# First units of an expert pair in halves, down weights by column halves and column chunks in turn

## The chip, the cores and the metric

The kernel runs on one core of one Trainium2 chip. The metric is the time of one execution on the device in microseconds (us), as the median of several runs. One further execution was profiled; all rows below are of that one.

## The reference

One layer of a transformer trunk for 384 tokens (128 context tokens, 256 latent ones) of width 2048, all in float32: modulated norm, a joint input projection for three groups of heads, attention, an output projection with a gated residual, and then a mixture of experts, which is the part that changes:

```python
g_top_p, g_top = top_k(softmax(h @ w_rg + b_rg), 1)           # 4 groups
e_logit, e_top = top_k((h @ w_re + b_re)[group g_top], 2)     # 2 of the 8 experts of a group
e_w = softmax(e_logit) * g_top_p
# 32 experts, each token goes to two; per expert e and its tokens x:
y = (silu(x @ w1[e]) * (x @ w3[e])) @ w2[e]                   # w1, w3: 2048 x 512, w2: 512 x 2048
out = x1 + g2 * sum over the token's two experts of e_w * y
```

Each expert has 12.6 MB of weights, all of which must be read once.

## The kernel before, in words

The stages ahead of the experts take the first 728 us or so. Then the tokens of each expert are put into items of up to 64 tokens, and items are worked in pairs: expert A fills rows 0 to 63 of the output partitions and expert B rows 64 to 127, so each step of a pair is two matmuls (one for each expert), and a float32 matmul shows as two instructions. There are 16 pairs in this run. The first is written out by hand with weights in 24 units of 1 MiB, and it is `moe0` in the code. The other 15 use 12 units of 2 MiB each, six slots of the tile `ring`, slot = unit % 6: units 0 to 3 are w1 (rows j = 0 to 7 of A and of B, then j = 8 to 15), 4 to 7 are w3 likewise, 8 to 11 are w2 (f = 0 and 1 of A and of B, then f = 2 and 3). A partition of a unit of w1 holds 8 steps j of 512 columns, 16 KB; one of w2 holds 2 rows f of 2048 columns, 16 KB, taken out of 32 KB in memory. Fourteen pairs are a hardware loop over m, the last is written out behind it.

Who does what in a pair:

- SyncE issues the loads in the order of the units and ahead of each waits until the slot is free (`moe_free`, lines 811 to 819; the loop, lines 876 to 882). Landing adds 16 to `big_full` of the slot, on which TensorE waits (`moe_arrived`).
- TensorE: `up` (lines 1376 to 1392) makes h1 and h3, 16 steps j each, and waits for two units when j is 0 or 8. From j = 5 of w1 on, one "back" of the pair before stands behind every second step (12 in all, line 1297): it spreads that pair's result over the tokens, three bfloat16 matmuls each on parts that ACT and DVE split off. Then `turn_next` transposes the gathered rows of the next pair, `turn_act` the activations, and the down-projection (lines 1410 to 1426) runs with f outside and the four column chunks c of 512 inside, one PSUM bank for each chunk. A chunk is complete after f = 3, and `y_full` counts it.
- ACT and DVE read h1, h3 and the complete chunks (`front`, `parts`), and GpSimd gathers the token rows of the pair after the next with an indirect DMA.

Behind the loop, the last pair (lines 1429 to 1454) has f = 0 and 1 for all chunks first, and then for each chunk f = 2 and 3, followed by the last backs of the chunk before (`last_back`, line 1402, float32, three matmuls a chunk on tiles that DVE has gated). DVE adds a strip to the residual for each, and SyncE stores it in pieces of 256 KB.

The lines that set the present order of the down-projection:

```python
for f in range(4):
    ua, ub = 8 + f // 2 * 2, 9 + f // 2 * 2
    if f % 2 == 0:
        moe_arrived(ua, m)
        moe_arrived(ub, m)
    for c in range(4):
        for h, u in enumerate((ua, ub)):
            mm = pe.matmul(y_ps[c][64 * h:64 * h + 64, :], act_t[:, f, 64 * h:64 * h + 64],
                           big_cut(slot_of(u), (2, D))[:, f % 2, c * 512:(c + 1) * 512], ...)
```

Of the kernel before, what the change touches and what calls it, by code (L numbers as in the profile page):

```python
# [18 lines left out]
I32 = mybir.dt.int32  # L19
# [5 lines left out]
P = 128  # L25
# [31 lines left out]
SCRATCH = 8192  # L57
BACKS = 4 * TILES
# [297 lines left out]
def by_units(w_mod, b_mod, w_in, w_o):  # L356
# [15 lines left out]
def build(nc, ins, outs):  # L372
# [54 lines left out]
    with ExitStack() as ctx:  # L427
# [22 lines left out]
        n_items = sb("n_items", [1, 1], I32)  # L450
# [209 lines left out]
        extra_full = [sem(f"extra_full{i}") for i in range(EXTRA[1] - EXTRA[0] - 1)]  # L660
        extra_free, strip_scaled = sem("extra_free"), sem("strip_scaled")
# [23 lines left out]
        def unit_source(u, e=0):  # L685
# [31 lines left out]
            w = ins["w2"][0][bass.ds(e, 1)]  # L717
            return w.rearrange("e (p j) n -> p (e j) n", j=4)[:, 2 * half:2 * half + 2, :], (2, D)
# [82 lines left out]
        moe_done = {3: (h1_full, 1), 7: (h3_full, 1), 11: (y_full, 4)}  # L801
# [26 lines left out]

        @block.sync
        def _(sp):  # L830
            for t in range(TILES):
# [36 lines left out]
            for u in range(MOE_UNITS):  # L868
# [5 lines left out]
                src, shape = unit_source(("moe", u), e[u % 2])  # L874
                sp.dma_start(big_cut(slot_of(u), shape), src).then_inc(big_full[slot_of(u)], 16)
            with sp.Fori(0, n) as m:
                e = [sp.value_load(expert_of[0:1, bass.ds(2 * m + 4 + c, 1)], min_val=0, max_val=EXPERTS - 1)
                     for c in range(2)]
                for u in range(MOE_UNITS):
                    sp.wait_ge(*(moe_free(u + BIG, m) if u < BIG else moe_free(u - BIG, m + 1)))  # L880
                    src, shape = unit_source(("moe", u), e[u % 2])
                    sp.dma_start(big_cut(slot_of(u), shape), src).then_inc(big_full[slot_of(u)], 16)
# [12 lines left out]
        def _(pe):  # L895
# [464 lines left out]
            for f in range(4):  # L1360
                ua, ub = 16 + 2 * f, 17 + 2 * f
                first_arrived(ua)
                first_arrived(ub)
                for c in range(4):
                    if f == 0 and c == 2:
                        pe.wait_ge(xt_read_a, 4)
                        pe.wait_ge(xt_read_v, 4)
                    for h, u in enumerate((ua, ub)):
                        mm = pe.matmul(y_ps[c][64 * h:64 * h + 64, :], act_t[:, f, 64 * h:64 * h + 64],  # L1369
                                       first_place(u)[:, c * 512:(c + 1) * 512], start=(f == 0), stop=(f == 3))  # L1370
                        if u == FIRST_UNITS - 1:
                            mm.then_inc(y_full, 1)
                        elif c == 3 and u in first_no:
                            mm.then_inc(slot_free[ring_slot(first_no[u])], 1)

            def up(m):
# [29 lines left out]
            with pe.Fori(0, n) as m:  # L1406
# [3 lines left out]
                for f in range(4):  # L1410
# [4 lines left out]
                    for c in range(4):  # L1415
                        if f == 0 and c == 2:
                            pe.wait_ge(xt_read_a, m * 2 + 6)
                            pe.wait_ge(xt_read_v, m * 2 + 6)
                        for h, u in enumerate((ua, ub)):
                            mm = pe.matmul(y_ps[c][64 * h:64 * h + 64, :], act_t[:, f, 64 * h:64 * h + 64],  # L1420
                                           big_cut(slot_of(u), (2, D))[:, f % 2, c * 512:(c + 1) * 512],
                                           start=(f == 0), stop=(f == 3))
                            if f == 3 and u in moe_done:
                                mm.then_inc(y_full, 1)
                            elif f % 2 and c == 3:
# [6 lines left out]
            def last_down(c, f):  # L1432

                for h in range(2):
                    mm = pe.matmul(y_ps[c][64 * h:64 * h + 64, :], act_t[:, f, 64 * h:64 * h + 64],  # L1435
                                   big_cut(slot_of(8 + f // 2 * 2 + h), (2, D))[:, f % 2, c * 512:(c + 1) * 512],
                                   start=(f == 0), stop=(f == 3))
                return mm

            moe_arrived(8, n)  # L1440
            moe_arrived(9, n)
            for f in range(2):
                for c in range(4):
                    last_down(c, f)
            moe_arrived(10, n)
            moe_arrived(11, n)
            for c in range(4):
                last_down(c, 2)
                last_down(c, 3).then_inc(y_full, 1)
                if c == 1:  # L1450
                    pe.wait_ge(w_ready, n + 2)
                if c:
                    last_back(n, c - 1)
# [967 lines left out]
```

## Time and profile before

| what | us |
|---|---|
| median of 3 runs | 1681.74 (1680.48 to 1683.66) |
| the profiled execution | 1681.13 |
| its span in the profile | 1679.3 |
| TensorE busy with matmuls | 1574.7 (94%) |
| DVE, ACT, GpSimd busy | 737.8, 281.0, 102.5 |

The span is the time from the first to the last instruction of the profiled execution; 1.8 us of its time lie around it. Busy times of several engines overlap. In the rows PE is TensorE, SPq the DMA-issuing queue of SyncE, and L1387 is line 1387 of the kernel: L1387 and L1346 are matmuls of the up-projection, L1420, L1369 and L1435 those of the down-projection, L1297 and L1402 the backs. All weights of the experts appear as `ring<-in_w`.

### The profile page before, as it was taken

How to read it: one execution, taken by the hardware profiler on the slowest of the kernel's cores; microseconds unless marked ns; L12 is line 12 of the kernel's file. 1: busy time of each engine (PE TensorE's matmuls, PEld its weight loads, DVE VectorE, ACT ScalarE, POOL GpSimd, SP SyncE). 2: the span in 40 equal slices, each digit the busy share in tenths (PEclk: the TensorE clock that was granted, in tenths of full speed). 3: DMA queues.
4: the chain of work that ended last, by engine and by line, in shares of the span. 5: the costliest groups of instructions: out<-in, count | busy, mean ns of one | idle time of the engine just before them, and what ended most of it. 6: DMA issues, size and time to landing. Idle time of an engine off the chain costs nothing.

```text
span 1679.3 us, 18083 instructions
## 1 busy us (share of the span) xinstructions
PE 1574.7 (94%) x6570; PEld 648.0 (39%) x6615; DVE 737.8 (44%) x1392; ACT 281.0 (17%) x744; POOL 102.5 (6%) x189
## 2 busy tenths in 40 slices
PE   6999999999999999999999899899989989989998
PEld 3446555544434444443332332333233233233323
DVE  3583333113255993344444445444434434544444
ACT  3014222112132000011101111110110111011010
POOL 1002100000022001010000000000000000000000
PEclk9999999999999999999999999999999999999999
DMA  9993345526199765699999999999999999999996
GB/s 394 420 415 130 117 187 223 206 107 251 57 380 415 278 262 202 234 376 426 424 429 428 428 428 427 425 428 426 427 428 422 426 428 424 429 425 428 425 426 250
DMA packets 60109, 581.93 MB, mean 347 GB/s; under 512 B 8993, under 2 KB 9953, under 8 KB 15179
## 3 DMA queue, kind: packets, MB, share of 16 engines
q1 hardware_dynamic: 52832, 557.34, 80.0%
q0 software_dynamic: 5936, 23.23, 3.6%
q10 hardware_dynamic: 1296, 0.77, 0.2%
q8 instruction: 27, 0.44, 0.1%
q14 instruction: 18, 0.15, 0.0%
HBM read 584.07 MB, written 7.05 MB: 352 GB/s over the span
## 4 chain that ended last, share of the span: by engine, by line
PE 68%; DMA 16%; DVE 4%; issue 2%; ACT 1%; SPq 0%; POOL 0%; ACTq 0%
PE bank L1387 24%; DMA ring<-in_w 16%; PE bank L1131 13%; PE bank L1297 7%; PE bank L1109 7%; PE bank L1420 3%; DVE r L1920 2%; PE bank L1004 2%; PE bank L1222 2%; PE bank L1346 2%; PE bank L1283 1%; PE bank L1435 1%; PE bank L1369 1%; PE bank L1197 1%; PE bank L1205 1%
## 5 line engine op out<-in xcount | busy, mean ns | idle before, releaser
L1387 PE MATMUL bank<-ring,r 128*64 128x512 f32 x1920 | 466.3, 615 | 45.3 <-DMA ring<-in_w 45.3
L1387 PEld LDWEIGHTS bank<-ring,r 128*64 128x64 f32 x1920 | 128.9, 139 | 300.6 <-issue 300.6
L2147 DVE TENSOR_TENSOR bank<-bank,r 128x512 f32<-128x512 f32 x180 | 126.0, 700 | 262.8 <-PE bank L1297 262.8
L1131 PE MATMUL bank<-ring,r 128*128 128x384 f32 (+2 forms) x672 | 225.4, 494 | 0.0
L1420 PE MATMUL bank<-ring,mod_row 128*64 128x512 f32 x896 | 195.8, 593 | 8.0 <-ACT mod_row L1655 7.9
L1109 PE MATMUL bank<-ring,r 128*128 128x512 f32 x384 | 170.0, 595 | 0.0
L1131 PEld LDWEIGHTS bank<-ring,r 128*128 128x128 f32 x672 | 123.6, 190 | 90.9 <-issue 43.2
L1297 PE MATMUL bank<-r 128*128 128x512 bf16 x495 | 137.6, 382 | 7.2 <-issue 7.2
L2149 DVE TENSOR_TENSOR r<-r,bank 128x512 f32<-128x512 f32 x180 | 123.6, 687 | 6.2
L1420 PEld LDWEIGHTS bank<-ring,mod_row 128*64 128x64 f32 x896 | 75.1, 137 | 119.1 <-issue 108.9
L1297 PEld LDWEIGHTS bank<-r 128*128 128x128 bf16 x540 | 38.0, 97 | 167.4 <-DVE r L2149 97.4
L1109 PEld LDWEIGHTS bank<-ring,r 128*128 128x128 f32 x384 | 71.1, 191 | 79.5 <-issue 79.4
L2170 DVE TENSOR_SCALAR gains<-bank,w_now 128x512 f32<-128x512 f32 x30 | 22.5, 751 | 175.3 <-PE bank L1420 162.3
L951 PE MATMUL bank<-r 128*128 128x512 f32 (+1 forms) x192 | 78.6, 558 | 5.1 <-DMA r<-in_w_cq 5.1
L2003 DVE TENSOR_REDUCE small<-bank 128x1 f32<-128x384 f32 (+1 forms) x48 | 22.5, 468 | 127.9 <-PE bank L1197 77.3
L1920 DVE SCALAR_TENSOR_TENSOR r<-ring,csil,r 128x2048 f32<-128x2048 f32 x32 | 74.3, 2349 | 6.3 <-DMA r<-in_b_mod 5.7
L1948 DVE SCALAR_TENSOR_TENSOR r<-r,small,gains 128x128 f32<-128x128 f32 (+2 forms) x91 | 27.4, 343 | 109.7 <-POOL small L2265 100.7
L1644 ACT ACTIVATE r<-bank 128x512 f32<-128x512 f32 x30 | 17.9, 595 | 301.7 <-PE bank L1283 301.7
L1764 DVE CUSTOM_DVE_ANT_0 r<-ring,r 128x2048 bf16<-128x2048 f32 x24 | 56.4, 2351 | 1.3
L1525 ACT ACTIVATE r<-bank 128x128 f32<-128x128 f32 (+1 forms) x76 | 21.0, 285 | 210.4 <-PE bank L1131 195.8
L1650 ACT ACTIVATE gain_row<-bank 128x512 f32<-128x512 f32 x16 | 9.6, 597 | 275.1 <-PE bank L1387 261.4
L951 PEld LDWEIGHTS bank<-r 128*128 128x128 f32 x192 | 35.6, 193 | 47.5 <-issue 32.5
(291 smaller groups left out, 1245.5 us busy)
## 6 DMA issues: line engine op xcount, KB each, us to landing
ring<-in_w SPq DMA_DIRECT2D x180, 2048.0 KB, 17.5
ring<-in_w_mod SPq DMA_DIRECT2D x64, 1024.0 KB, 11.6
ring<-in_w SPq DMA_DIRECT2D x18, 1024.0 KB, 9.0
ring<-in_w_scale SPq DMA_DIRECT2D x16, 1024.0 KB, 26.9
ring<-in_w_shift SPq DMA_DIRECT2D x16, 1024.0 KB, 26.7
ring<-in_w_o SPq DMA_DIRECT2D x16, 1024.0 KB, 6.3
r<-mod_d POOLq DMA_DIRECT2D x8, 1024.0 KB, 8.5
ring<-in_w_aq SPq DMA_DIRECT2D x8, 768.0 KB, 14.2
```

The source lines that it names most:

```text
L951: mm = pe.matmul(early_bank[3 * c + t][:, 0:w], h_t[:, k, t * P:(t + 1) * P], early_w[c][i % 2][:, jj, :], start=(k == 0), stop=(k == KD - 1))
L1004: mm = pe.matmul(mod_ps[32 * q:32 * q + 2, :], csil[:, k, 0:2], ring[:, ring_slot(m), q * 512:(q + 1) * 512], start=(k == 0), stop=(k == K ...
L1109: mm = pe.matmul(acc[acc_of(a)][:, :], qo[:, t, k, :], wu[:, j, :], start=(k == 0), stop=(k == KD - 1))
L1131: mm = pe.matmul(acc[acc_of(a)][:, 0:w], h_t[:, k, t * P:(t + 1) * P], wu[:, j, :], start=(k == 0), stop=(k == KD - 1))
L1222: mm = pe.matmul(out, v, prob_t[u % 2][:, i, :] if g == "C" else prob_ab[batch_of(u) % 2][:, i, :], start=(i == 0), stop=(i == len(tiles) ...
L1297: mm = pe.matmul(y_ps[k % 4][:, :], of_token[:, t * P:(t + 1) * P], y_part[:, n_part, c, :], start=(n_part == 0), stop=(n_part == 2))
L1387: mm = pe.matmul(ps[64 * c:64 * c + 64, :], xg_t[:, j, 64 * c:64 * c + 64], big_cut(slot_of(u), (8, 512))[:, j % 8, :], start=(j == 0), st ...
L1420: mm = pe.matmul(y_ps[c][64 * h:64 * h + 64, :], act_t[:, f, 64 * h:64 * h + 64], big_cut(slot_of(u), (2, D))[:, f % 2, c * 512:(c + 1) * ...
L1764: last = v.tensor_tensor_reduce(junk_s, w, cond_all[:, c, :], 1.0, b_shift[:, k:k + 1], ALU.mult, ALU.add, mod_t[:, 1, k, c:c + 1])
L1920: last = v.scalar_tensor_tensor(out=g2_sum[:, c, :], in0=ring[:, ring_slot(m), :], scalar=csil[:, k, c:c + 1], in1=g2_sum[:, c, :], op0=AL ...
L2147: v.tensor_tensor(ps[:, :], ps[:, :], g2b[:, min(t, 1), cols], ALU.mult).then_inc(strip_scaled, 1)
L2149: return v.tensor_tensor(x1[:, t, cols], x1[:, t, cols], ps[:, :], ALU.add)
```

## The change

The weights w2 are laid out anew in memory on the host, outside the timed execution: for each expert two dense blocks of 2 MiB, one for columns 0 to 1023 and one for 1024 to 2047, in each of which a partition holds chunk after chunk and in a chunk f after f. A unit of w2 is then a column half with all four f. The down-projections run with c outside and f inside, and `y_full` counts each chunk when it is complete, so unit 9 and the odd units of the first pair have `y_full` for the sign that they are free. Units 0 and 1 of each of the 15 pairs are loaded in halves, in the order 0a, 1a, 0b, 1b; the first halves have semaphores of their own (`half_full`, the reused `early_in`), and `up` waits for them at j = 0 and for the whole units at j = 4. SyncE's loop ends one pair earlier, and the last pair's loads are written out behind it, w2 in eight transfers of 1 MiB, chunk by chunk, counted in `last_full`. The last pair's down-projection waits for each chunk and runs chunk by chunk.

```diff
+    down = w2[0].reshape(EXPERTS, P, 4, 2, 2, 512)
+    out["w2"] = down.transpose(0, 3, 1, 4, 2, 5).reshape(EXPERTS, 2, P, 2 * D)
...
-                return ins["w2"][0][n % 2].rearrange("(p j) n -> p j n", j=4)[:, (n - 16) // 2, :], (D,)
+                c = (n - 16) // 2
+                return ins["w2"][n % 2, c // 2][:, c % 2 * D:c % 2 * D + D], (D,)
...
-            w = ins["w2"][0][bass.ds(e, 1)]
-            return w.rearrange("e (p j) n -> p (e j) n", j=4)[:, 2 * half:2 * half + 2, :], (2, D)
+            w = ins["w2"][bass.ds(e, 1), half]
+            return w.rearrange("e p (c n) -> p (e c) n", c=2), (2, D)
+
+        def last_source(e, c):
+
+            w = ins["w2"][bass.ds(e, 1), c // 2]
+            return w.rearrange("e p n -> p (e n)")[:, c % 2 * D:c % 2 * D + D]
...
-            elif u == FIRST_UNITS - 1:
-                frees[m] = (y_full, 4)
+            elif u > 16 and u % 2:
+                frees[m] = (y_full, (u - 15) // 2)
...
-        moe_done = {3: (h1_full, 1), 7: (h3_full, 1), 11: (y_full, 4)}
+        moe_done = {3: (h1_full, 1, 1), 7: (h3_full, 1, 1), 9: (y_full, 4, 2), 11: (y_full, 4, 4)}
...
-                full, n = moe_done[u]
-                return full, m * n + 2 * n
+                full, each, at = moe_done[u]
+                return full, m * each + each + at
...
+            def load_big(u, e):
+
+                src, shape = unit_source(("moe", u), e[u % 2])
+                if u > 1:
+                    sp.dma_start(big_cut(slot_of(u), shape), src).then_inc(big_full[slot_of(u)], 16)
+                    return
+                sp.dma_start(big_cut(slot_of(u), shape)[:, 0:4, :], src[:, 0:4, :]).then_inc(half_full[u], 16)
+                for c in range(2 * u):
+                    src, shape = unit_source(("moe", c), e[c])
+                    sp.dma_start(big_cut(slot_of(c), shape)[:, 4:8, :], src[:, 4:8, :]).then_inc(big_full[slot_of(c)], 16)
...
-            with sp.Fori(0, n) as m:
+                load_big(u, e)
+            before_last = sp.value_load(n_items[0:1, 1:2], min_val=HALF_PAIR - 3, max_val=MAX_PAIRS - 3)
+            with sp.Fori(0, before_last) as m:
...
-                    src, shape = unit_source(("moe", u), e[u % 2])
-                    sp.dma_start(big_cut(slot_of(u), shape), src).then_inc(big_full[slot_of(u)], 16)
+                    load_big(u, e)
...
+            for u in range(8):
+                sp.wait_ge(*(moe_free(u + BIG, before_last) if u < BIG else moe_free(u - BIG, before_last + 1)))
+                load_big(u, e)
+            for c in range(4):
+                for h in range(2):
+                    if c % 2 == 0:
+                        sp.wait_ge(*moe_free(2 + c + h, before_last + 1))
+                    sp.dma_start(big_cut(slot_of(8 + c // 2 * 2 + h), (2, D))[:, c % 2, :],
+                                 last_source(e[h], c)).then_inc(last_full[c], 16)
...
-                        if j % 8 == 0:
+                        if w == 0 and j == 0:
+                            for c in range(2):
+                                pe.wait_ge(half_full[c], m * 16 + HALF_FULL + 16)
+                        elif j % 8 == (4 if w == 0 and j < 8 else 0):
                             moe_arrived(ua, m)
                             moe_arrived(ub, m)
...
-                for f in range(4):
-                    ua, ub = 8 + f // 2 * 2, 9 + f // 2 * 2
-                    if f % 2 == 0:
-                        moe_arrived(ua, m)
-                        moe_arrived(ub, m)
-                    for c in range(4):
-                        if f == 0 and c == 2:
-                            pe.wait_ge(xt_read_a, m * 2 + 6)
-                            pe.wait_ge(xt_read_v, m * 2 + 6)
-                        for h, u in enumerate((ua, ub)):
+                for c in range(4):
+                    if c == 2:
+                        pe.wait_ge(xt_read_a, m * 2 + 6)
+                        pe.wait_ge(xt_read_v, m * 2 + 6)
+                    if c % 2 == 0:
+                        moe_arrived(8 + c, m)
+                        moe_arrived(9 + c, m)
+                    for f in range(4):
+                        for h in range(2):
+                            u = 8 + c // 2 * 2 + h
                             mm = pe.matmul(y_ps[c][64 * h:64 * h + 64, :], act_t[:, f, 64 * h:64 * h + 64],
-                                           big_cut(slot_of(u), (2, D))[:, f % 2, c * 512:(c + 1) * 512],
+                                           big_cut(slot_of(u), (2, D))[:, c % 2, f * 512:(f + 1) * 512],
                                            start=(f == 0), stop=(f == 3))
-                            if f == 3 and u in moe_done:
+                            if f == 3 and h == 1:
                                 mm.then_inc(y_full, 1)
...
+            def last_down(c):
+
+                pe.wait_ge(last_full[c], 16 + 2 * 16)
+                for f in range(4):
...
+            last_down(0)
+            last_down(1)
+            pe.wait_ge(w_ready, n + 2)
+            last_back(n, 0)
+            last_down(2)
+            last_back(n, 1)
+            last_down(3)
+            last_back(n, 2)
             last_back(n, 3)
```

The diff is cut: the first pair's down-projection is turned in the same way as that of the loop, and `n_items` gets a second value, one less than the first.

## Rows read from the trace of the kernel before

**Rows 1.** The page, section 2: what the DMA engines moved in 40 slices.

```profile
GB/s 394 420 415 130 117 187 223 206 107 251 57 380 415 278 262 202 234 376 426 424 429 428 428 428 427 425 428 426 427 428 422 426 428 424 429 425 428 425 426 250
```

**Rows 2.** Waits of TensorE and SyncE's queue: us in total, times, longest.

```profile
PE bank L1387 <- DMA ring<-in_w: 45.3, 20, 3.4
PE bank L1297 <- issue: 7.2, 45, 0.2
...
SPq L882 <- PE bank L1387: 522.4, 56, 12.0
```

**Rows 3.** Timeline, TensorE: start, us, instructions [idle before, releaser].

```profile
889.87 7.07 PE L1387 MATMUL bank<-ring,r 128*64 128x512 f32 x24 [3.06 <-DMA ring<-in_w]
...
949.88 5.37 PE L1387 MATMUL bank<-ring,r 128*64 128x512 f32 x24 [2.77 <-DMA ring<-in_w]
...
959.66 1.94 PE L1387 MATMUL bank<-ring,r 128*64 128x512 f32 x8 [1.03 <-DMA ring<-in_w]
...
992.57 14.26 PE L1420 MATMUL bank<-ring,mod_row 128*64 128x512 f32 x64 [0.56 <-ACT mod_row L1655]
1009.88 7.07 PE L1387 MATMUL bank<-ring,r 128*64 128x512 f32 x24 [3.06 <-DMA ring<-in_w]
...
1608.61 5.37 PE L1387 MATMUL bank<-ring,r 128*64 128x512 f32 x24 [1.59 <-DMA ring<-in_w]
...
1618.38 1.94 PE L1387 MATMUL bank<-ring,r 128*64 128x512 f32 x8 [1.03 <-DMA ring<-in_w]
```

**Rows 4.** Windows of 20 us; last three columns: granted clock, DMA share, GB/s.

```profile
940.00:960.00 20.00, 16.04 (x73) 5.68 (x72) 9.36 (x14) 6.25 (x10) 0.00 (x0) 1.00 1.01 430
...
1000.00:1020.00 20.00, 16.79 (x69) 5.80 (x66) 8.06 (x12) 6.25 (x10) 0.00 (x0) 0.91 1.01 430
...
1040.00:1060.00 20.00, 19.27 (x96) 7.85 (x95) 7.08 (x13) 1.47 (x3) 1.19 (x2) 1.00 1.00 419
```

**Rows 5.** DMA queues from 940 to 1000 us.

```profile
DMA packets 1887, 25.65 MB, mean 428 GB/s; under 512 B 296, under 2 KB 296, under 8 KB 296
```

**Rows 6.** DMA issues of the whole run: size of each, median us to landing.

```profile
ring<-in_w SPq DMA_DIRECT2D x180, 2048.0 KB, 17.5
...
out_y_prompt<-r SPq DMA_DIRECT2D x4, 256.0 KB, 2.4
```

**Rows 7.** Windows ahead of the loop, columns as in rows 4.

```profile
730.00:760.00 30.00, 30.00 (x154) 12.17 (x150) 6.89 (x28) 1.49 (x3) 2.53 (x5) 1.00 1.01 423
...
40.00:60.00 20.00, 20.00 (x78) 8.23 (x77) 4.87 (x4) 0.00 (x0) 0.64 (x1) 0.98 1.02 423
100.00:120.00 20.00, 18.10 (x61) 8.73 (x58) 15.53 (x16) 2.65 (x6) 3.31 (x6) 1.00 1.02 410
```

**Rows 8.** The chain that ended last, its end: start, us, what.

```profile
1650.38 7.09 PE bank L1435 x32
...
1657.49 3.65 PE bank L1435 x16
1661.14 2.77 PE bank L1402 x6
1663.91 1.87 PE bank L1435 x8
...
1670.42 5.36 PE bank L1402 x12
```

**Rows 9.** Line L882 from 1590 to 1640 us: ns, min, median, max.

```profile
L882 SPq DMA_DIRECT2D ring<-in_w x12: 333/333/381, 1590.2 to 1639.1; - x12
...
DMA to landing us min/median/max: 13.1/16.8/20.8
```

**Rows 10.** Timeline, DVE, the gating of one chunk of the last pair.

```profile
1659.46 1.41 DVE L2211 SCALAR_TENSOR_TENSOR r<-bank,w_now,r 128x512 f32<-128x512 f32 x2 [8.79 <-PE bank L1435]
```

**Rows 11.** Windows of 5 us in the last stage, columns as in rows 4.

```profile
1650.00:1655.00 5.00, 4.62 (x22) 1.96 (x24) 0.67 (x3) 0.30 (x1) 0.00 (x0) 1.00 0.83 354
1655.00:1660.00 5.00, 4.99 (x24) 1.78 (x22) 0.54 (x1) 0.00 (x0) 0.00 (x0) 1.00 0.09 36
```

More of the change, by code:

```diff
@@ L57 @@
 SCRATCH = 8192
+HALF_FULL = 64
 BACKS = 4 * TILES
@@ L353, in units_of, with by_units @@
     return [("in", name, i) for i in range(KD // rows_of(name))]
-def by_units(w_mod, b_mod, w_in, w_o):
+def by_units(w_mod, b_mod, w_in, w_o, w2):
     out = {}
@@ L449, in build @@
         small = sb("small", [P, 90])
-        n_items = sb("n_items", [1, 1], I32)
+        n_items = sb("n_items", [1, 2], I32)
         gat_now = sb("gat_now", [P, 1], I32)
@@ L660, in build @@
         extra_full = [sem(f"extra_full{i}") for i in range(EXTRA[1] - EXTRA[0] - 1)]
+        last_full = extra_full[0:4]
         extra_free, strip_scaled = sem("extra_free"), sem("strip_scaled")
@@ L880, in _ @@
                     sp.wait_ge(*(moe_free(u + BIG, m) if u < BIG else moe_free(u - BIG, m + 1)))
-                    src, shape = unit_source(("moe", u), e[u % 2])
-                    sp.dma_start(big_cut(slot_of(u), shape), src).then_inc(big_full[slot_of(u)], 16)
+                    load_big(u, e)
+            e = [sp.value_load(expert_of[0:1, bass.ds(2 * before_last + 4 + c, 1)], min_val=0, max_val=EXPERTS - 1)
+                 for c in range(2)]
+            for u in range(8):
[7 more added lines that the diff above has]
+                                 last_source(e[h], c)).then_inc(last_full[c], 16)
             for k in range(BACKS):
@@ L1409, in _ @@
                 turn_act(m)
-                for f in range(4):
-                    ua, ub = 8 + f // 2 * 2, 9 + f // 2 * 2
-                    if f % 2 == 0:
-                        moe_arrived(ua, m)
-                        moe_arrived(ub, m)
-                    for c in range(4):
-                        if f == 0 and c == 2:
-                            pe.wait_ge(xt_read_a, m * 2 + 6)
-                            pe.wait_ge(xt_read_v, m * 2 + 6)
-                        for h, u in enumerate((ua, ub)):
+                for c in range(4):
+                    if c == 2:
+                        pe.wait_ge(xt_read_a, m * 2 + 6)
[4 more added lines that the diff above has]
+                    for f in range(4):
+                        for h in range(2):
+                            u = 8 + c // 2 * 2 + h
                             mm = pe.matmul(y_ps[c][64 * h:64 * h + 64, :], act_t[:, f, 64 * h:64 * h + 64],
-                                           big_cut(slot_of(u), (2, D))[:, f % 2, c * 512:(c + 1) * 512],
+                                           big_cut(slot_of(u), (2, D))[:, c % 2, f * 512:(f + 1) * 512],
                                            start=(f == 0), stop=(f == 3))
-                            if f == 3 and u in moe_done:
+                            if f == 3 and h == 1:
                                 mm.then_inc(y_full, 1)
-                            elif f % 2 and c == 3:
+                            elif f == 3 and c % 2:
                                 mm.then_inc(big_free[slot_of(u)], 1)
@@ L1430, in _ @@
             turn_act(n)
[L1432 to L1453, printed above, removed]
+            def last_down(c):
+                pe.wait_ge(last_full[c], 16 + 2 * 16)
+                for f in range(4):
+                    for h in range(2):
+                        mm = pe.matmul(y_ps[c][64 * h:64 * h + 64, :], act_t[:, f, 64 * h:64 * h + 64],
+                                       big_cut(slot_of(8 + c // 2 * 2 + h), (2, D))[:, c % 2, f * 512:(f + 1) * 512],
+                                       start=(f == 0), stop=(f == 3))
+                mm.then_inc(y_full, 1)
+            last_down(0)
[6 more added lines that the diff above has]
+            last_back(n, 2)
             last_back(n, 3)
@@ L2131, in _ @@
             v.tensor_scalar(n_items[:, 0:1], n_extra[0:1], float(HALF_PAIR - 2), None, ALU.add)
+            v.tensor_scalar(n_items[:, 1:2], n_extra[0:1], float(HALF_PAIR - 3), None, ALU.add)
             v.wait_ge(tab_full, 1)
@@ L2408 @@
     arrays = {f"in_{n}": np.ascontiguousarray(inputs[n]) for n in IN_NAMES
-              if n not in ("w_in", "w_o") and n not in dict(GAIN_ROWS)}
-    for n, a in by_units(inputs["w_mod"], inputs["b_mod"], inputs["w_in"], inputs["w_o"]).items():
+              if n not in ("w_in", "w_o", "w2") and n not in dict(GAIN_ROWS)}
+    for n, a in by_units(inputs["w_mod"], inputs["b_mod"], inputs["w_in"], inputs["w_o"],
+                         inputs["w2"]).items():
         arrays[f"in_{n}"] = np.ascontiguousarray(a)
```

16 lines of the change are left out of this document (8 added, 8 removed).

## The prediction

> **What bounds the kernel now.** The page first: one core, and in nearly every slice of the second half of the span 422 to 429 GB/s are moved [rows 1], while TensorE is busy nearly all the time as well. Shares can't say which of the two sets the pace of the expert pairs, so I went on to the waits. TensorE waits for weights in the up-projection 20 times, 45.3 us in all; the queue of SyncE in its turn waits for TensorE to free slots, 522.4 us in the biggest of its groups [rows 2]. So each waits for the other, and the list alone would allow a loop in which a shorter wait of TensorE starts transfers earlier. The timeline of TensorE settles the pace [rows 3]: the first matmul of a pair starts at 889.87, 949.88 and 1009.88, every 60.0 us, whatever TensorE did in between (the wait before it was 3.06, 2.77 and 3.06 us, the first 24 matmul instructions took 7.07 or 5.37 us). A pace that takes no notice of TensorE is that of the other side. The windows by 20 us agree: DMA share 1.00 to 1.01 and 419 to 430 GB/s in each [rows 4]. One pair is 12 units of 2 MiB, 25.17 MB, with the gathered rows 25.65 MB between 940 and 1000 [rows 5]; at 428 GB/s that is 59.9 us. And a unit lands 17.5 us after its issue (median) while 2 MiB take 4.9 us at 428 GB/s, so over three are in flight: the queue's waits for slots don't empty the DMA engines [rows 6].
>
> So from about 730 us, where the DMA share reaches 1.0 [rows 7], until the last landing that TensorE waits for, time is bytes over rate. That landing is at 1618.2 us: the second unit-pair of the last pair (units 2 and 3, needed at j = 8), where TensorE waits 1.03 us [rows 3]. The chain of waits from there on holds no DMA: the steps from j = 8 with the backs of the pair before, the transposition, the 64 instructions of the down-projection, last backs to 1675.78, then one DVE strip and its store [rows 8]. The span is therefore (last wait ends, 1618.38) + 60.9 us in which TensorE or what it must wait for is never short of weights.
>
> **The change part by part.**
>
> *First units in halves.* Units 0 and 1 (both experts' w1, first half) come as 1 MiB pieces, first halves of both, then second halves. Both units together take 4.19 MB / 428 = 9.8 us, so the first halves land 4.9 us before unit 1 lands now. Take the pair at 1009.88: TensorE ended the down-projection at 992.57 + 14.26 = 1006.83 and waited for a landing at about 1009.7. The first halves would be there at 1004.8: no wait. The 16 instructions of j = 0 to 3 take about 3.5 us (5.37 for 24), to 1010.5, and the second halves are there at 1009.7: no wait either. From the first matmul to the end of j = 7 TensorE needs 959.66 - 1.03 - 949.88 = 8.75 us, so it stands at j = 8 at 1006.98 + 8.75 = 1015.7. There units 2 and 3 are next, and they land at 959.5 + 60 = 1019.5 as now. So the wait is moved, not removed: 2.77 + 1.03 = 3.80 us in two places become about 3.8 us in one. After it everything is at its old time; worth 0. The cover is the DMA engines' work itself; were it gone, the wait's whole length would be won (a rival below).
>
> *What else follows the earlier start.* The backs of the pair before (from j = 5) come some 4.9 us earlier in that pair and need split parts that ACT and DVE can finish only after y_full; the next edit gives the first y_full earlier, so nothing stands there. Slots of units 0 and 1 come free some 3 us earlier; the queue has over three units in flight already, 0.
>
> *More and smaller transfers.* Two more issues per pair on SyncE: an issue instruction is 0.33 us, and 12 issues spread over 49 us, 1590.2 to 1639.1 [rows 9], so the queue has room. The second half of unit 0 now also waits for unit 7's slot (one 0.2 us matmul later), with 13.1 us or more from issue to landing in which earlier transfers run [rows 9]. What isn't hidden is any loss of rate on the pieces of 8 KB per partition where there were 16 KB. Bytes: units 0 and 1 of 15 pairs, 62.9 MB, 147 us at 428 GB/s. The nearest rows are the stretch where the very first pair's 1 MiB units (8 KB per partition) load at full share: 423 GB/s [rows 7], against 428 for the 2 MiB units [rows 5]. At 423 the loss is 147 x (428/423 - 1) = 1.7 us; but in that stretch two broadcasts on the software queue run as well, so some of the difference is theirs. Lower end 0. I take the middle, +0.8 us. The Trainium skill ("DMA: Bandwidth & Descriptors", Bandwidth) gives a 1 MB transfer 341 GB/s and 16 MB 425 GB/s and asks to batch; by 341 on the halves the sum would be 147 x (428/341 - 1) = 37 us higher. The trace doesn't agree for transfers in a full queue: the 1 MiB units ran at 423 there.
>
> *w2 by column halves, from memory.* Each unit stays 2 MiB in 16 KB runs per partition, now dense instead of every second 16 KB. The 126 MB of 15 pairs are 294 us of transfer. No row of before has dense 16 KB runs. The first pair's w1 units (8 KB out of every 32 KB) at 423 and the early dense scale and shift units (8 KB, dense) at 423 are equal [rows 7], so I take 0; the bounds are one per cent either way on 294 us, -2.9 and +2.9 us.
>
> *Column chunks in turn.* The same 64 instructions with the same weight loads; y_full for chunk 0 and 1 comes 7 to 10 us earlier, for chunk 3 when it did, so ACT and DVE start on the parts earlier and end the last ones as before. The first two units of w2 are free halfway as before (after 32 of 64 instructions), the others at the end. TensorE doesn't wait for the parts now: what its backs wait for in front of them is issue, 0.2 us at most [rows 2]. 0. The wait for the readers of the transposed rows at chunk 2 comes 5 us later in the stage than it did: 0, since none is seen there now.
>
> *SyncE's last pair written out behind the loop, one more value loaded.* A few register instructions and one load on a queue with 13 us of transfers under way, 0.
>
> *The last pair's down-projection.* Before: 32 + 16 instructions, then back 0, 8, back 1, 8, backs 2 and 3: 7.09 + 3.65 + 2.77 + 1.87 + 2.77 + 1.87 + 5.36 = 25.38 us, without a gap [rows 8]. After: chunks 0 and 1 (7.1), back 0 (2.77), chunk 2 (3.65), back 1 (2.77), chunk 3 (3.65), backs 2 and 3 (5.36) = 25.3. Is it still gapless? Chunks 0 and 1 are at 1654.0 and 1657.5; DVE gates chunk 0 in 1.41 us [rows 10], done 1655.5, so back 0 at 1657.5 finds it with 2 us in hand. Back 3 at 1673.0 needs chunk 3, full at 1670.3, gated at 1671.8. The weights: the last unit lands about 1654 (354 GB/s in 1650 to 1655, then 36 [rows 11]); chunk 2 is wanted at 1660.1 and chunk 3 at 1666.5. So the stores of the first columns leave some 3.5 us earlier and the last ones when they did: -0.1 us. These 8 KB pieces lie behind the last wait for weights and cost nothing.
>
> Sum: 0 + 0.8 + 0 + 0 + 0 - 0.1 = +0.7 us on the profiled execution, 1681.13 (span 1679.3 and 1.8 around it): 1681.8. The median of the runs, 1681.74, is 0.6 above that execution, so 1682.4.
>
> **Rivals.**
>
> *The split pays in full.* If the transfers were paced by slots that TensorE frees, each wait before the first matmul would be won: thirteen, of which rows 3 show the first (3.06) and the last (1.59), with a sum of 38.0 us: 1644 us. For it: the queue does wait for TensorE, 522.4 us in one group [rows 2]. Against it: DMA share 1.0 in the windows [rows 4] and the even 60.0 us. It would need DMA gaps that no window shows. Chance 0.03.
>
> *Dense w2 is faster.* It decides from 3.4 / 294 = 1.15% on these units; at 1.5% -4.4 us and with +0.7 it gives 1678. For it: only that w2 is a third of the bytes. Against: 423 and 423. 0.06.
>
> *Small pieces cost more (the other side).* From a rate below 428 / (1 + 3.4/147) = 418 GB/s on the halves it is slower; at 410, the lowest full-share window of the early stage [rows 7], 6.5 us, 1688. For it: that row. Against: it holds transfers of much smaller pieces too. 0.09. Its extreme is a fixed cost per transfer paid in the DMA engines: a 256 KB store takes 2.4 us from issue to landing [rows 6], of which the bytes are 0.6, so 1.8 us x 2 x 15 = +54 us, 1736; that the 1 MiB units run at 423 speaks against it. 0.01. The Trainium skill ("DMA: Bandwidth & Descriptors", Anatomy of one DMA) has such a fixed cost of about 2.0 us and puts most of it down to the receipt of the last write; the store's 1.8 us agree with the size, and no row shows it taken from a full queue's rate.
>
> *The clock falls in the last pair.* After waits of 3.06 us the first 24 instructions took 7.07 instead of 5.37 us and the granted clock was 0.91 in that window; after 2.77 and 1.59 us they took 5.37 [rows 3, 4]. With one wait of 3.8 us this now happens right behind j = 8; inside the loop it shortens the next wait and costs nothing, in the last pair it lengthens the chain by 1.7 us: 1684.1. There the wait should be 2.6 us at most (1.59 + 1.03), below those that were followed by a fall. 0.15, and still within 0.2%.
>
> *The last pair stalls on a chunk.* If a chunk came 12 us late; nothing in the queue does that. Under 0.01.
>
> **How the numbers follow.** 0.2% of the median, 3.4 us, is about what a measurement of this kernel tells from no change (the three runs spread 3.2 us). The forecast, 1682.4, has 0.63, its own range 1680.6 to 1684.2 from the bounds of the small pieces (0 to 1.7) and of the runs' spread. With the fallen clock (0.15) no measurable change has 0.78. Faster: 0.03 + 0.06 and 0.01 for the unforeseen, 0.10. Slower: 0.09 + 0.01 and 0.02 for a wait that I don't see, 0.12. The rest of w2's bounds widens the range a little on both sides: 1679.3 to 1685.6.
>
> **What would show it.** In the profile after: the first matmul of a pair right behind the down-projection and no wait there; one wait of 2 to 4 us per pair at j = 8; 60.0 to 60.2 us from one such wait's end to the next; DMA share 1.0; in the last stage no gap of TensorE and the end at 1676. A period under 59.5 us, or DMA share below 1 at any place, would make the prediction wrong; a period of 60.3 or more would be the small pieces.

## The result, and the profile after

The changed kernel took 1686.64 us (median of 20 runs, 1683.92 to 1689.98), the kernel before 1683.38 us in the 20 runs beside them (1680.48 to 1686.75). The ratio is 1.0017, 95% interval 1.0011 to 1.0023: slower by 2.9 us, 1.9 to 3.9. The forecast was +0.7 us and 1682.4, with a range to 1685.6. Of the 4.2 us between forecast and result, 2.2 are the effect of the change (+2.9 instead of +0.7), 1.6 are the reference (1681.74 was the median of three runs; over 20 it is 1683.38), and the rest, 0.4, is the difference between ratio and medians.

The profiled execution took 1685.34 us, with a span of 1683.5 (before: 1681.13 and 1679.3). Timeline of TensorE, four of the 14 waits for weights in it, the first three and the last; all 14 stand at j = 8 (start, us, instructions, [idle before, releaser]):

```profile
842.10 1.94 PE L1424 MATMUL bank<-ring,r 128*64 128x512 f32 x8 [1.30 <-DMA ring<-in_w]
...
902.26 3.68 PE L1424 MATMUL bank<-ring,r 128*64 128x512 f32 x8 [4.44 <-DMA ring<-in_w]
...
962.40 3.20 PE L1424 MATMUL bank<-ring,r 128*64 128x512 f32 x8 [1.85 <-DMA ring<-in_w]
...
1622.76 1.94 PE L1424 MATMUL bank<-ring,r 128*64 128x512 f32 x8 [1.90 <-DMA ring<-in_w]
```

The waits of [rows 3] at the start of a pair are gone, and one of 1.3 to 4.5 us at j = 8 stands in for them. The list of waits puts a sum to it, 42.5 us in 14 waits for 45.3 us in 20 of [rows 2]:

```profile
PE bank L1424 <- DMA ring<-in_w: 42.5, 14, 4.5
```

From the first such wait's end to the last one's are 1622.76 - 842.10 = 780.66 us; in before it was 1618.38 - 839.64 = 778.74 us (the last is in [rows 3], the first is this row of the same timeline), so +1.9 us in 13 pairs.

```profile
839.64 1.94 PE L1387 MATMUL bank<-ring,r 128*64 128x512 f32 x8 [1.05 <-DMA ring<-in_w]
```

The DMA queues from 940 to 1000 us, beside [rows 5], show what is new there: 280 more packets for no more bytes. Of them 31 are small ones, under 512 B. The other 249 fit the two units of the pair that now come in halves: each of their 128 partitions gets two runs of 8 KB (a run is what lies in one piece in memory and goes to one partition) instead of one of 16 KB, 256 runs more.

```profile
DMA packets 2167, 25.56 MB, mean 426 GB/s; under 512 B 327, under 2 KB 327, under 8 KB 327
...
ring<-in_w SPq DMA_DIRECT2D x4, 1024.0 KB, 14.0
```

The end of the chain, beside [rows 8]:

```profile
1654.76 7.09 PE bank L1474 x32
1661.84 2.77 PE bank L1439 x6
1664.62 3.58 PE bank L1474 x16
1668.20 2.77 PE bank L1439 x6
1670.97 3.58 PE bank L1474 x16
1674.56 5.36 PE bank L1439 x12
```

From 1654.76 to 1679.92 are 25.2 us without a gap (25.4 before), and from the last wait for weights to the end of the span 60.7 us (60.9 before). The new order of the last pair does what was forecast for it.

The other 2.5 us between the two profiled executions lie ahead of the first wait at j = 8, which ends at 842.10 instead of 839.64, and 2.3 of them lie ahead of all changed code. The last 16 of the matmuls that pick the first pair's rows out of the tokens ("picking matmuls" from here on) start that much later, first in before, then in the changed kernel:

```profile
719.33 7.11 PE L1090 MATMUL bank<-r,cst 128*128 128x512 f32 x16
...
721.63 7.11 PE L1124 MATMUL bank<-r,cst 128*128 128x512 f32 x16
```

In the 8 picking matmuls ahead of these the granted clock fell. Windows of 5 us (columns as in rows 4), first of the changed kernel, then of before:

```profile
710.00:715.00 5.00, 3.89 (x31) 3.27 (x30) 3.04 (x9) 1.32 (x3) 1.46 (x2) 0.88 0.93 324
715.00:720.00 5.00, 5.00 (x9) 2.42 (x9) 4.02 (x16) 0.00 (x0) 0.00 (x0) 0.50 0.95 377
```

```profile
715.00:720.00 5.00, 4.79 (x22) 2.29 (x22) 4.09 (x16) 0.00 (x0) 0.28 (x1) 1.00 1.00 392
```

At 0.50 of full speed (the lower of the clock's two levels, 1.2 GHz) this stage ends later, and SyncE's next weight loads, which come behind a wait for it, start 2.3 us later too, first in before, then in the changed kernel:

```profile
731.97 9.33 SPq L856 DMA_DIRECT2D ring<-in_w  x6
...
734.27 9.33 SPq L879 DMA_DIRECT2D ring<-in_w  x6
```

Since everything behind is bound by transfers, the delay stays to the end.

### The profile page after: what moved, and what is told of

Same layout as the page of the kernel before. It is cut to its first block, busy times and chain, and to the rows that moved or that the text cites. A ratio compares the mean times of both kernels' runs of the same rounds, so it can differ in the third digit from the quotient of the medians.

```text
span 1683.5 us, 18288 instructions
## 1 busy us (share of the span) xinstructions
PE 1590.6 (94%) x6615; PEld 652.5 (39%) x6615; DVE 737.6 (44%) x1393; ACT 281.0 (17%) x744; POOL 102.4 (6%) x189
## 4 chain that ended last, share of the span: by engine, by line
PE 69%; DMA 15%; DVE 4%; issue 1%; ACT 1%; SPq 0%; POOL 0%; ACTq 0%
PE bank L1424 21%; DMA ring<-in_w 15%; PE bank L1165 13%; PE bank L1331 7%; PE bank L1143 7%; PE bank L1457 6%; DVE r L1953 2%; PE bank L1038 2%; PE bank L1317 2%; PE bank L1256 2%; PE bank L1380 2%; PE bank L1474 1%; PE bank L1403 1%; PE bank L1124 1%; PE bank L1231 1%
## 5 line engine op out<-in xcount | busy, mean ns | idle before, releaser
L1424 PE MATMUL bank<-ring,r 128*64 128x512 f32 x1920 | 469.7, 618 | 42.5 <-DMA ring<-in_w 42.5
L1331 PE MATMUL bank<-r 128*128 128x512 bf16 x540 | 150.7, 389 | 0.0
```

The lines of the kernel that those rows point to most:

```text
L1331: mm = pe.matmul(y_ps[k % 4][:, :], of_token[:, t * P:(t + 1) * P], y_part[:, n_part, c, :], start=(n_part == 0), stop=(n_part == 2))
L1424: mm = pe.matmul(ps[64 * c:64 * c + 64, :], xg_t[:, j, 64 * c:64 * c + 64], big_cut(slot_of(u), (8, 512))[:, j % 8, :], start=(j == 0), st ...
```

## The experiments

Eleven further runs were made: nine more kernels, and both old ones once more. They ran on several chips; each ratio is against runs of before made beside that kernel. So that the chance of the early stage doesn't blur the profiles, three stretches are read from each: from the start of the last 16 picking matmuls (about 720 us) to the end of the span ("pick to end"); from the end of the first wait at j = 8 to the end of the last ("the distance"); and from there to the end of the span. An entry is empty where such a wait is missing or the stretch was not read. In the three profiles with long runs the distance differs by 0.33 us at most, in the three with the split by 0.03 us, so it tells 2 us apart where single spans don't.

| kernel | span | pick to end | first to last wait at j = 8 | behind it | ratio to before (95%) |
|---|---|---|---|---|---|
| before | 1679.3 | 959.8 | 778.7 | 60.9 | |
| before, again | 1680.8 | 959.7 | 778.5 | 60.8 | |
| the change | 1683.5 | 961.7 | 780.7 | 60.7 | 1.0017 (1.0011 to 1.0023) |
| the change, again | 1684.6 | 963.7 | 780.7 | 62.4 | 1.0024 (1.0010 to 1.0037) |
| units whole | 1684.2 | 959.9 | 778.9 | 60.8 | 1.0008 (0.9995 to 1.0020) |
| split alone | 1684.8 | 962.2 | 780.7 | 60.9 | 1.0018 (1.0004 to 1.0031) |
| runs of 8 KB | 1686.1 | 964.2 | 782.8 | 60.6 | 1.0018 (1.0009 to 1.0027) |
| all in halves | 1693.6 | 968.9 | 786.9 | 60.7 | 1.0046 (1.0033 to 1.0060) |
| fewer bytes | 1619.9 | 899.0 | no waits | | 0.9622 (0.9607 to 0.9637) |
| early backs | 1678.0 | 958.3 | none at j = 8 | | 0.9989 (0.9980 to 0.9997) |
| early backs, old order | 1687.6 | 963.2 | none at j = 8 | | 1.0026 (1.0013 to 1.0040) |
| early backs in the change | 1683.5 | 960.8 | | 58.1 | 1.0008 (0.9999 to 1.0017) |
| cut by partitions | 1988.0 | | | | 1.1826 (1.1801 to 1.1852) |

**The change once more.** No edit.

> The changed kernel as it is, for a second profile. Theory A (two causes: the pieces of units 0 and 1 cost 1.9 us over 13 pairs; the fall of the clock at 714 to 721 us, ahead of the experts, was chance): the time is some 3 us above before as in the result, the distance from the first to the last wait for units 2 and 3 is again about 780.7 us (778.7 in before), and the end of the first such wait is anywhere from 839.6 to 842.1, by whether the clock falls ahead of it. Rival B (something in the change brings the fall at 714 us about): it is there again, and the first wait ends near 842.

The distance came back to 0.03 us (780.69), so the loop's share is no noise. The fall of the clock ahead of the experts was there again (0.66 from 715 to 720 us), and the first wait ended at 841.53, so this run alone can't rule out rival B; the second profile of before, below, does. Here the clock also fell where the prediction's clock rival had put it, behind the last wait (0.72 from 1622 to 1625 us). Timeline of TensorE:

```profile
841.53 1.94 PE L1424 MATMUL bank<-ring,r 128*64 128x512 f32 x8 [1.61 <-DMA ring<-in_w]
...
1622.22 2.62 PE L1424 MATMUL bank<-ring,r 128*64 128x512 f32 x8 [3.47 <-DMA ring<-in_w]
```

The last wait was 3.47 us, the 8 instructions behind it took 2.62 instead of 1.94 us, later ones were slow as well, and the stretch behind is 62.4 instead of 60.7 us: about 1.7 us, the rival's price.

**Units whole, the rest of the change kept.**

```diff
-                if u > 1:
-                    sp.dma_start(big_cut(slot_of(u), shape), src).then_inc(big_full[slot_of(u)], 16)
-                    return
-                sp.dma_start(big_cut(slot_of(u), shape)[:, 0:4, :], src[:, 0:4, :]).then_inc(half_full[u], 16)
...
+                sp.dma_start(big_cut(slot_of(u), shape), src).then_inc(big_full[slot_of(u)], 16)
```

> Units 0 and 1 come whole again, w2 by column halves and the column order stay. Theory A: the 1.9 us of the loop are gone, distance from first to last wait for units 2 and 3 back at 778.7 us, time within 1 us of before. Rival C (the dense layout of w2 or the order of chunks is what slows the transfers): distance stays at 780.7 us and the time stays some 3 us above before.

```profile
844.57 1.94 PE L1415 MATMUL bank<-ring,r 128*64 128x512 f32 x8 [1.04 <-DMA ring<-in_w]
...
1623.43 1.94 PE L1415 MATMUL bank<-ring,r 128*64 128x512 f32 x8 [1.04 <-DMA ring<-in_w]
```

Distance 778.86 us: with whole units the loop is as fast as in before, so neither the dense w2 nor the chunk order costs or gives anything there that shows. The timed ratio, 1.0008 (0.9995 to 1.0020), can't tell it from before, nor by itself from the change.

**The split alone, in the kernel before.** The mirror image: `load_big` and `half_full` put into before, w2 and the down-projections left.

> The kernel before with units 0 and 1 in halves, w2 and the order of the down-projection as in before. Theory A: distance 780.7 us, time 2 to 3 us above before. Rival C: distance 778.7 us, time as before.

```profile
843.23 1.94 PE L1402 MATMUL bank<-ring,r 128*64 128x512 f32 x8 [1.64 <-DMA ring<-in_w]
...
1623.91 1.94 PE L1402 MATMUL bank<-ring,r 128*64 128x512 f32 x8 [2.00 <-DMA ring<-in_w]
```

Distance 780.68 us and a ratio of 1.0018 (1.0004 to 1.0031). All that the loop loses comes with the split, and rival C has fallen on both sides.

**Units 0 and 1 cut by partitions.**

```diff
-                sp.dma_start(big_cut(slot_of(u), shape)[:, 0:4, :], src[:, 0:4, :]).then_inc(half_full[u], 16)
+                sp.dma_start(big_cut(slot_of(u), shape)[0:64], src[0:64]).then_inc(half_full[u], 16)
...
-                    sp.dma_start(big_cut(slot_of(c), shape)[:, 4:8, :], src[:, 4:8, :]).then_inc(big_full[slot_of(c)], 16)
+                    sp.dma_start(big_cut(slot_of(c), shape)[64:128], src[64:128]).then_inc(big_full[slot_of(c)], 16)
```

> The changed kernel, but units 0 and 1 are cut by partitions (0 to 63, then 64 to 127), so that there are as many transfers as in the change but each partition's run is 16 KB again; TensorE waits for both parts at j = 0. Theory A in the form 'shorter runs cost': distance 778.7 us, time within 1 us of before. Theory A in the form 'each further transfer costs': distance 780.7 us, time some 2 to 3 us above before.

Neither: 1988.84 us, 18% slower. It can't decide between runs and transfers, since something far bigger sits on top. Windows of this kernel, one while such pieces load and one while whole units do:

```profile
920.00:940.00 20.00, 9.74 (x32) 3.17 (x32) 3.37 (x6) 3.12 (x5) 0.00 (x0) 0.68 1.01 210
...
960.00:980.00 20.00, 20.00 (x87) 5.31 (x84) 10.71 (x16) 0.60 (x1) 0.00 (x0) 1.00 1.00 425
```

The DMA engines are busy all the time in both, and move half as much while transfers that cover 64 partitions are under way.

**The kernel before, once more.** No edit.

> The kernel before once more, for a second profile. Theory A: the clock falls between 713 and 725 us in this kernel too in some executions (it did in four of the five profiles so far, not in the one of before); with it the first wait for units 2 and 3 ends at 841 to 845 us instead of 839.6, and the distance to the last one is 778.7 to 778.9 us again. Rival B (the change brings the fall): no fall, 839.6 us.

Theory A, windows of 5 us of this execution:

```profile
715.00:720.00 5.00, 5.00 (x14) 2.77 (x14) 3.38 (x16) 0.00 (x0) 0.56 (x1) 0.66 0.98 360
```

The clock fell to 0.66 in the kernel before as well, and the first and last wait at j = 8 are these:

```profile
841.43 1.94 PE L1387 MATMUL bank<-ring,r 128*64 128x512 f32 x8 [1.04 <-DMA ring<-in_w]
...
1619.96 1.94 PE L1387 MATMUL bank<-ring,r 128*64 128x512 f32 x8 [1.03 <-DMA ring<-in_w]
```

The distance is 778.53 us. So the fall at 715 us isn't the change's. Over all 13 profiles the 8 picking matmuls took 3.68 us in three (before, runs of 8 KB, early backs) and 4.97 to 6.53 us in the other ten; the profile that the prediction was made from was one of the rarer kind. (This execution took 1682.68 us, below the median of before all the same.)

**Runs of 8 KB in whole transfers.**

```diff
+                if n < 4:
+                    return w.rearrange("e (p b a i) n -> p (e b) a (i n)", b=2, a=2, i=4)[:, :, half, :], (2, D)
...
+                            at = j if w else j // 8 * 4 + j % 8 // 4 * 8 + j % 4
-                            mm = pe.matmul(ps[64 * c:64 * c + 64, :], xg_t[:, j, 64 * c:64 * c + 64],
+                            mm = pe.matmul(ps[64 * c:64 * c + 64, :], xg_t[:, at, 64 * c:64 * c + 64],
```

> Units 0 to 3 whole, 2 MiB each, but gathered so that a partition has two runs of 8 KB instead of one of 16 KB (units 0 and 1 hold j = 0 to 3 and 8 to 11, units 2 and 3 the rest): twice as many short runs as the change has and no further transfer. If the length of the runs costs, 0.3 us a pair and a distance of 778.8 + 3.8 = 782.6 us; if each further transfer costs, 778.8 us and the time of the kernel with whole units.

The first and the last wait at j = 8:

```profile
842.63 1.94 PE L1418 MATMUL bank<-ring,r 128*64 128x512 f32 x8 [1.19 <-DMA ring<-in_w]
...
1625.47 1.94 PE L1418 MATMUL bank<-ring,r 128*64 128x512 f32 x8 [1.15 <-DMA ring<-in_w]
```

782.84 us, 4.1 above the mean of the three profiles with long runs (778.7), with not one transfer more. The length of the runs costs. From the pick to the end it is 4.4 us more than in before; the timed ratio stands for 3.0 us (1.5 to 4.5), so it shows that short runs cost but leaves the size to the profiles.

**All eight units of w1 and w3 in halves.**

```diff
+                for i in (0, 4):
+                    sp.dma_start(big_cut(slot_of(u), shape)[:, i:i + 4, :],
+                                 src[:, i:i + 4, :]).then_inc(big_full[slot_of(u)], 16)
```

The diff is cut: the counts that TensorE waits for are raised to match, and it waits for whole units at j = 0 and 8 as in before.

> All eight units of w1 and w3 in two transfers of 1 MiB one behind the other, waits as with whole units: eight further transfers per pair instead of two. Theory A: four times the 0.15 us a pair, distance 778.8 + 7.8 = 786.6 us, time some 9 us above before. Rival D (what cost was the order 0a, 1a, 0b, 1b or the moved wait, not the pieces): 779 us and the time of before.

```profile
846.03 1.94 PE L1421 MATMUL bank<-ring,r 128*64 128x512 f32 x8 [1.19 <-DMA ring<-in_w]
...
1632.92 1.94 PE L1421 MATMUL bank<-ring,r 128*64 128x512 f32 x8 [1.18 <-DMA ring<-in_w]
```

786.89 us, +8.2. The three kernels are three doses of the same thing, 2, 4 and 8 units in short runs a pair, over 13 pairs. Per pair and unit they cost 1.95/(13 x 2) = 0.075, 4.13/(13 x 4) = 0.079 and 8.18/(13 x 8) = 0.079 us. The last has a further transfer for each such unit and the one before it none, and the price is the same: it is all the runs', and a further transfer in a full queue costs nothing that shows. How the runs lie in memory doesn't show either: in a transfer they are 16 KB apart in the one and 32 KB in the other. The mean rate from 850 to 1600 us goes the same way: 427 GB/s in before and with whole units, 425, 424 and 422 with two, four and eight units in short runs. Rival D has fallen.

**Fewer bytes.** Half of w1's first half is left out in each of the 15 pairs, and TensorE uses the other half twice.

```diff
+                if u < 2:
+                    sp.dma_start(big_cut(slot_of(u), shape)[:, 0:4, :], src[:, 0:4, :]).then_inc(big_full[slot_of(u)], 16)
+                    return
```

> Units 0 and 1 whole in the waits, but only their first half is loaded and TensorE uses it twice (half of the first half of w1 of each pair is left out): 4.9 us less of transfer per pair, all else as with whole units. Theory A (transfers set the pace, TensorE has 3.8 us of slack per pair): the waits for weights vanish and the pair takes what TensorE needs, 56.2 us; time some 52 us below before. Rival E (the loop of waits between TensorE and the queue sets the pace): the pair stays near 60 us.

1621.09 us, 3.8% or 64 us less, more than the 52 us expected. Timeline of TensorE, the start of two up-projections:

```profile
941.83 5.35 PE L1418 MATMUL bank<-ring,r 128*64 128x512 f32 x24
...
997.16 5.35 PE L1418 MATMUL bank<-ring,r 128*64 128x512 f32 x24
```

The next starts at 1052.49, so a pair takes 55.3 us; the list of waits of this kernel has no entry for weights of the pairs. Fewer bytes shorten the pair, as theory A has it, and rival E has fallen. What TensorE needs for a pair was put 0.9 us too high (56.2). No fall of the clock is left in the pairs, since no wait is (1.00 from 940 to 1060 us, where before has 0.91 in [rows 4]); that this is the 0.9 us was not tested. The transfers are no longer far behind in this kernel: 23.55 MB a pair at 428 GB/s are 55.0 us (an estimate from [rows 5]), and the DMA share is still 1.01. A share of 1.0 alone doesn't tell who sets the pace.

**Early backs.** The only wait that can be won is that of the last pair, and only by work that needs no weights. Made from the kernel with whole units.

```diff
-                if k == 0:
-                    pe.wait_ge(y_read_a, i * 2 + 2)
-                    pe.wait_ge(y_read_v, i * 2 + 2)
+                if k in (0, 2):
+                    pe.wait_ge(y_read_a, i * 2 + 1 + k // 2)
+                    pe.wait_ge(y_read_v, i * 2 + 1 + k // 2)
...
+                back(m, 0)
+                back(m, 1)
                 for w, ps in enumerate((h1_ps, h3_ps)):
...
-                        if j % 2 and 4 <= KD * w + j < 28:
-                            back(m, (KD * w + j) // 2 - 2)
+                        if j % 2 and 2 <= KD * w + j < 22:
+                            back(m, (KD * w + j) // 2 + 1)
```

> Units whole, w2 by column halves, and the backs of the pair before three places earlier: backs 0 and 1 ahead of the first wait for weights, 2 to 4 before j = 8. They need no weights, so in the last pair they fill 2.25 us of the 2.5 us that TensorE waits there. Theory A (only what stands behind the last wait for weights counts): distance between first and last wait for units 2 and 3 stays 778.7 to 778.9 us, the chain from the last wait to the end shrinks from 60.8 to about 58.6 us, time 2 us below the kernel with whole units. Rival F (the backs wait for ACT's and DVE's parts, or DVE's strips become the limit): the waits only change their name, chain 60.8 us.

1681.21 us, ratio 0.9989 (0.9980 to 0.9997): faster than before by 1.9 us (0.5 to 3.4). From the pick to the end it is 958.3 us instead of 959.8. The chain's end shows that the last wait for weights is now the one at j = 0 (1610.23). At j = 8 there is none in any pair, so the distance and the chain behind it, of which the expectation spoke, can't be read here. The last down-projection and the last backs run without a gap, to 1674.46.

```profile
1589.22 20.88 DMA ring<-in_w
1610.10 0.14 issue
1610.23 3.65 PE bank L1417 x16
...
1649.30 7.09 PE bank L1467 x32
1656.39 2.77 PE bank L1432 x6
1659.16 3.58 PE bank L1467 x16
```

**Early backs in the kernel before**, f outside as it was.

> The kernel before with the backs three places earlier as in the run before, f outside and w2 as it was. The first y_full comes 9 us later than with chunks in turn, and the parts for back 0 are ready some 1.2 us behind the down-projection. Theory A: that still lies inside the wait for unit 1, chain from the last wait to the end 58.6 to 59.5 us, time 1 to 2 us below before. If the chunk order is what makes early backs possible, the chain stays near 60.8 us.

Slower than before, 1.0026. Two things are in its timeline, both of the order of the down-projection. The parts for back 0 come late (line 1297 waits for DVE), in every pair; and in the last pair f = 2 and 3 of all chunks need units 10 and 11 at 1661:

```profile
1614.20 1.24 PE L1297 MATMUL bank<-r 128*128 128x512 bf16 x5 [1.68 <-DVE r L2179]
...
1664.09 5.35 PE L1437 MATMUL bank<-ring,mod_row 128*64 128x512 f32 x16 [2.65 <-DMA ring<-in_w]
```

That wait is 2.65 us, and the 16 instructions behind it took 5.35 instead of 3.65 (granted clock 0.66 from 1664 to 1669 us): together 4.35 us in the stage that nothing covers. The last down-projection starts 1.0 us earlier, counted from the pick, than in before, and the two make up the 3.4 us by which pick to end grew (963.2 for 959.8). With chunks in turn (early backs, above) chunk 2 is wanted 2.8 us later behind a back, and chunks 0 and 1 need nothing of the last units. So the second half of the change (chunks in turn, with w2 laid out and loaded by them), worth nothing by itself, is what early backs stand on; which of its parts is needed was not tested apart. The expectation saw the first wait and not the second.

**Early backs in the changed kernel.**

> The changed kernel with the backs three places earlier. Theory A: the short runs still cost 2.0 us over the distance (780.7 us), the chain behind the last wait is about 58.6 us unless the clock falls; time about that of before.

Ratio 1.0008 (0.9999 to 1.0017); behind the last wait 58.1 us. The first wait at j = 8 is missing, so the distance can't be read, but both kernels with early backs and chunks in turn wait in the first and in the last down-projection. First this kernel, then early backs without the split:

```profile
883.96 7.09 PE L1459 MATMUL bank<-ring,mod_row 128*64 128x512 f32 x32 [2.78 <-DMA ring<-in_w]
...
1605.70 7.09 PE L1459 MATMUL bank<-ring,mod_row 128*64 128x512 f32 x32 [1.83 <-DMA ring<-in_w]
```

```profile
880.50 8.79 PE L1450 MATMUL bank<-ring,mod_row 128*64 128x512 f32 x32 [2.35 <-DMA ring<-in_w]
...
1600.44 7.09 PE L1450 MATMUL bank<-ring,mod_row 128*64 128x512 f32 x32 [1.83 <-DMA ring<-in_w]
```

That is 721.74 against 719.94 us, 1.8 us in 12 pairs, 0.075 us for each of two units a pair: the price of short runs a fourth time. The split's loss and the backs' gain about cancel.

## Why the prediction was wrong

- *Transfers set the pace.* Right: DMA share 1.0, 60.15 us per pair instead of 60.0, and fewer bytes is what shortens a pair.
- *The wait is moved, not removed.* Right: 14 waits at j = 8, 42.5 us in all for 45.3, none at the start of a pair. They last 1.3 to 4.5 us, where 2 to 4 were forecast.
- *Smaller transfers, +0.8 us with bounds of 0 and 1.7.* This is the step that failed, by size. It is 0.078 us for each unit in short runs, in 30 units 2.3 us, above the upper bound. The row behind the bound, 423 GB/s between 730 and 760 us, was not of short runs alone: 2 MiB units are issued from 744 on and move within it. From 730 to 745 us, nearly all ahead of them, it is 423 as well, so a rate read off one short window with other traffic in it was no bound in the first place. And halving its difference for the two broadcasts had nothing behind it. By 0.078 on 4.90 us the rate of short runs is 428/1.016 = 421 GB/s, an estimate. That the Trainium skill's 341 GB/s for a 1 MB transfer doesn't hold in a full queue was right.
- *w2 dense, 0.* Right: 778.86 with it and 778.74 and 778.53 without.
- *Chunks in turn, 0; the last pair's down-projection, -0.1 us.* Right in the changed kernel: 25.2 for 25.4 us, no gap. Two readings on the way were off, and nothing hung on them: by the count of instructions chunks 0 and 1 are complete 8 and 5 us earlier, not 7 to 10, and in before weights still moved until about 1656 us, not 1654.
- *The clock falls in the last pair*, given 0.15. It did in one of the three profiles with the split and the old backs (1.7 us), not in the two of before. Two claims behind the 0.15 were wrong: the wait was 3.47 us there and not 2.6 at most, and the length of a wait doesn't tell whether the clock falls (in the changed kernel 8 instructions took 3.20 us after a wait of 1.85 us, and 1.94 us after one of 3.10). By one in three it adds some 0.6 us, an estimate; 2.3 + 0.6 - 0.1 = 2.8 us beside a measured 2.9 (1.9 to 3.9). How often it falls in unprofiled runs stays open.
- *The reference.* The sum was set on a median of three runs, which was 1.6 us below that of 20, and on a profile without the fall at 715 us. The spread of three runs, 3.2 us, was taken for the kernel's; it is 6.3 us over 20. By the prediction's 0.2% bound the change counts as no difference, the case that had 0.78, but the effect is real and of the other case's sign: the rival "small pieces cost more" had the mechanism, with a price of its own that was too high.

## What to carry to other kernels

Where the period of a loop takes no notice of the waits in it and is that of its bytes, cutting a transfer to let the consumer start sooner only moved the wait here, and the shorter runs were paid in full. The place to win was behind the last landing that is waited for: take work that needs no transfer out of that stretch and put it into the waits ahead of it, and look at once which landing is late next. Before costing a change of 1 us, compare several profiles from an event ahead of it; one profile's span had 2.3 us of chance in a stage that the change doesn't touch.

## What the runs showed of the hardware

- Runs of 8 KB per partition instead of 16 KB cost 0.078 us per 2 MiB (doses of 0.075, 0.079 and 0.079). That is 128 more packets over 16 engines, 8 each, so 9.8 ns a packet by division; a further transfer costs nothing that shows beside it. Why a packet costs that stays open. The Trainium skill ("DMA: Bandwidth & Descriptors", Bandwidth, Measured) puts the floor of its 4 KB transfer, issued from GpSimd, down to about 10.5 ns a packet; the number is close, but no run here shows that it is the same cost. The same page of the Trainium skill has line rate from 512 B up (Specifications); the trace agrees only roughly, since from 8 to 16 KB the rate still rose by 1.6%.
- While transfers that cover partitions 0 to 63 or 64 to 127 were under way, 210 GB/s moved at a DMA share of 1.01 (920 to 940 us of that kernel), against 425 to 428 with transfers over 128 partitions, and the kernel was 18% slower.
- TensorE was slow behind waits for weights in 9 of the 14 cases of the changed kernel, 8 instructions taking 2.74 to 3.68 instead of 1.94 us: after all four waits of over 4 us, after some of 1.85 to 3.20 us, and not after others of 3.10 and 3.14 us. The granted clock goes with it: 0.50, its lower level (1.2 GHz), from 1322 to 1326 us after a wait of 3.17 us, and 1.00 (2.4 GHz) from 1022.5 to 1026 us after one of 3.10.
